# DeltaNet heads: the low weight part made from a negated high part and an accumulating transfer, in place of GpSimd's subtraction

## The reference

```
h = rmsnorm(x, norm_g)
proj = h @ w_in
(rq, rk, rv, rz, dq, dk, dv, dz, db, da, gr, gd) = split(proj)
o_r = retention(rope(rq), rope(rk), rv)      # normed, times silu(rz)
qkv = silu(causal_conv([dq, dk, dv], conv_w))
o_d = gated_deltanet(l2norm(q), l2norm(k), v, beta, g)   # normed, times silu(dz)
y = sigmoid(gr) * (o_r @ w_up_r) + sigmoid(gd) * (o_d @ w_up_d)
return x + y @ w_o
```

## Time and profile before

| | |
|---|---|
| median of 2 runs | 2645.55 us |
| span of the profiled execution, first to last instruction | 2644.2 us |
| TensorE busy | 2620.6 us (99%) |
| TensorE weight loads | 2238.1 us (85%) |
| VectorE busy | 1761.1 us (67%) |
| GpSimd busy | 798.6 us (30%) |
| ScalarE busy | 704.5 us (27%) |
| read from memory, written | 176.30 MB, 38.86 MB |

### The profile page before, as it was taken

How to read it: one execution, slowest core, us unless ns; L and a number is a source line. 1 busy time by engine, 2 the same in 40 slices (tenths; PEclk the granted TensorE clock), 3 DMA queues, 4 the chain that set the end, 5 groups by cost and what they waited for, 6 DMA issues and landing times.

```text
span 2644.2 us, 40210 instructions
## 1 busy us (share of the span) xinstructions
PE 2620.6 (99%) x14874; PEld 2238.1 (85%) x14874; DVE 1761.1 (67%) x3972; ACT 704.5 (27%) x1440; POOL 798.6 (30%) x451
## 2 busy tenths in 40 slices
PE   8999999999999999999999999999999999999998
PEld 6888888888888899888877888888888998898887
DVE  7878777877755555434577778777877555653333
ACT  5333333333311212200143333333332221231001
POOL 3123333333312212334512233332322122132453
PEclk9999999999999999999999999999999999999999
DMA  5321222122211112433533222222222111133344
GB/s 174 100 85 58 81 69 85 53 86 65 85 50 43 41 35 76 130 96 120 157 90 88 77 74 69 73 77 72 67 77 73 43 51 43 41 106 100 99 135 152
DMA packets 293416, 217.79 MB, mean 82 GB/s; under 512 B 31747, under 2 KB 246101, under 8 KB 292965
## 3 DMA queue, kind: packets, MB, share of 16 engines
q1 hardware_dynamic: 259620, 159.07, 20.9%
q10 hardware_dynamic: 33600, 56.15, 6.3%
HBM read 176.30 MB, written 38.86 MB: 81 GB/s over the span
## 4 chain that ended last, share of the span: by engine, by line
PE 92%; DVE 3%; DMA 2%; issue 1%; ACT 1%; SPq 0%; POOL 0%; ACTq 0%; DVEq 0%; POOLq 0%
PE dense_ps L866 23%; PE dense_ps L870 23%; PE dense_ps L868 23%; PE work L849 3%; PE dense_ps L890 2%; PE dense_ps L891 2%; PE dense_ps L892 2%; PE work L1145 1%; PE work L1182 1%; PE work L1202 1%; PE work L1121 1%; PE work L1104 1%; PE work L1171 1%; PE work L1195 1%; PE work L1156 1%
## 5 line engine op out<-in xcount | busy, mean ns | idle before, releaser
L866 PE MATMUL dense_ps<-act_hi,w_hi 128*128 128x512 f32 x2552 | 1048.3, 411 | 1.7 <-DVE w_lo L1797 0.8
L870 PE MATMUL dense_ps<-act_hi,w_lo 128*128 128x512 f32 x2552 | 998.4, 391 | 0.0
L868 PE MATMUL dense_ps<-act_lo,w_hi 128*128 128x512 f32 x2552 | 997.3, 391 | 0.0
L2579 POOL TENSOR_TENSOR w_lo<-w_raw,w_hi 128x1024 fp32r<-128x1024 f32 x162 | 400.1, 2470 | 1024.5 <-ACT w_hi L1429 582.7
L870 PEld LDWEIGHTS dense_ps<-act_hi,w_lo 128*128 128x128 f32 x2552 | 479.0, 188 | 105.8
L866 PEld LDWEIGHTS dense_ps<-act_hi,w_hi 128*128 128x128 f32 x2552 | 481.0, 188 | 86.9 <-POOL act_lo L2600 2.3
L868 PEld LDWEIGHTS dense_ps<-act_lo,w_hi 128*128 128x128 f32 x2552 | 481.5, 189 | 78.8 <-issue 0.5
L1973 DVE SCALAR_TENSOR_TENSOR arena<-arena,cols 128x512 f32<-128x512 f32 x288 | 244.3, 848 | 6.1
L1429 ACT ACTIVATE w_hi<-w_raw 128x1024 fp32r<-128x1024 f32 x94 | 99.1, 1054 | 330.5 <-PE dense_ps L870 310.5
L1419 ACT ACTIVATE arena<-dense_ps 128x512 f32<-128x512 f32 x96 | 57.2, 596 | 258.5 <-PE dense_ps L870 258.5
L849 PE MATMUL work<-mk,arena 128*128 128x128 f32 x768 | 112.1, 275 | 7.9 <-DMA arena<-in_x 7.9
(11 more groups left out here) (262 smaller groups left out, 4094.7 us busy)
## 6 DMA issues: line engine op xcount, KB each, us to landing
w_raw<-in_w_in SPq DMA_DIRECT2D x138, 512.0 KB, 3.8
arena<-l_scratch SPq DMA_DIRECT2D x64, 256.0 KB
arena<-gate_scratch ACTq DMA_DIRECT2D x64, 256.0 KB, 2.7
gate_scratch<-arena ACTq DMA_DIRECT2D x36, 256.0 KB, 2.0
w_raw<-in_w_out SPq DMA_DIRECT2D x18, 512.0 KB, 3.7
o_scratch<-arena ACTq DMA_DIRECT2D x32, 256.0 KB, 2.2
w_raw<-in_w_up_dn SPq DMA_DIRECT2D x16, 512.0 KB, 3.6
arena<-o_scratch ACTq DMA_DIRECT2D x32, 256.0 KB, 3.7
```

The lines of the kernel that those rows point to most:

```text
L866: eng.matmul(dense_ps[:, to, :], w_hi[:, slot, k, :], hi[:, k, seg], start=(k == 0), stop=False)
L868: eng.matmul(dense_ps[:, to, :], w_hi[:, slot, k, :], lo[:, k, seg], start=False, stop=False)
L870: mm = eng.matmul(dense_ps[:, to, :], w_lo[:, slot, k, :], hi[:, k, seg], start=False, stop=(k == KT - 1))
L2579: eng.tensor_tensor(w_lo[:, slot, :, :], w_from[second][:, :, :], w_hi[:, slot, :, :].bitcast(F32), ALU.subtract)\
```

## The change

In the units `even` and `odd` GpSimd's subtraction is replaced. ACT writes two things: `w_hi`, as before, and then, in a second instruction, `w_lo` from the same `w_raw` with scale -1. As `w_lo` has the short form too, that is the negated high part. GpSimd then issues a transfer that reads the raw block from memory again (`w_in`) and adds it to `w_lo` in place, which leaves raw - hi. It signals `w_lo_ok` as soon as the transfer is issued, which frees `w_raw` for the next load; the landing is told by two semaphores of their own (`w_added`, by the parity of the block), for which TensorE waits before the block's first matmul. `w_hi_ok` now counts two to a block, and all that waits for it is changed to match; the units `first`, `even_last` and `odd_last` and all other blocks keep the subtraction. Three signals of the gates are put on one semaphore (`Later`).

```diff
-        w_hi_ok, w_lo_ok = signal("w_hi_ready", 1), signal("w_lo_ready", 1)
+        w_hi_ok, w_lo_ok = signal("w_hi_ready", 2), signal("w_lo_ready", 1)
+        w_added = [plain("w_lo_added_even"), plain("w_lo_added_odd")]
...
-        b_tokps = signal("ba_tokens_psum", 1)
-        b_gcps, b_rowps, b_rows = signal("gc_psum", 1), signal("rows_psum", 1), signal("rows_ready", 2)
+        b_tokps, b_rows = signal("ba_tokens_psum_then_gc_then_rows", 3), signal("rows_ready", 2)
+        b_gcps, b_rowps = Later(b_tokps, 1), Later(b_tokps, 2)
...
                                 eng.wait_ge(w_lo_ok.sem, w_lo_ok.after(g, 1))
+                                if 1 <= g % NBLK - BLK_HEADS <= 6 * (DH - 1):
+                                    eng.wait_ge(*added(g))
...
+                def split_signed(g, slot):
+
+                    eng.wait_ge(w_in_ok.sem, w_in_ok.after(g, 16))
+                    eng.wait_ge(dense_ok[1].sem, dense_ok[1].after(g, -1))
+                    eng.wait_ge(w_hi_ok.sem, w_hi_ok.after(g, 0))
                     eng.activation(w_hi[:, slot, :, :], w_raw[:, :, :], ACT.Copy).then_inc(w_hi_ok.sem, 1)
+                    eng.activation(w_lo[:, slot, :, :], w_raw[:, :, :], ACT.Copy, scale=-1.0).then_inc(w_hi_ok.sem, 1)
...
+            def add_w(g, slot, col):
+
+                eng.wait_ge(w_hi_ok.sem, w_hi_ok.after(g, 2))
+                eng.dma_start(w_lo[:, slot, :, :], w_src(l, w_in, col), accum_op=ALU.add)\
+                   .then_inc(w_added[g % 2], 16)
+                eng.sem_inc(w_lo_ok.sem, 1)
...
                             if idx == BLK_RET + 2 and kind == "even_last":
                                 split_v(l, 0, 0)
+                            elif kind in ("even", "odd"):
+                                add_w(g + idx, idx % 2, head_column(h, idx - BLK_HEADS))
                             elif kind != "first" and not is_v(idx):
                                 split_w(g + idx, idx % 2)
```

More of the change, by code:

```diff
@@ L81, with __init__, Later @@
 class Signal:
-    def __init__(self, handle, per):
-        self.sem, self.per = handle, per
+    def __init__(self, handle, per, before=0):
+        self.sem, self.per, self.count = handle, per, before
     def after(self, t, k):
-        return t * self.per + (self.per + k)
+        return t * self.per + (self.per + self.count + k)
+def Later(first, before):
+    return Signal(first.sem, first.per, first.count + before)
 def constants():
@@ L621, in l_source, with head_column, added @@
                 .to_broadcast([NB, BASE, 2 * BASE * BASE])
+        def head_column(h, j):
+            if j == 6:
+                return DK0 + (h + 2) * P if h < DH - 2 else DZ0 + (h + 1) * P
+            return (None, DZ0 + h * P, DQ0 + (h + 1) * P, DV0 + (h + 1) * P, GD0 + (h + 1) * P, GR0 + (h + 1) * P)[j]
+        def added(g):
+            l, q = g // NBLK, g % NBLK - BLK_HEADS
+            assert 1 <= q <= 6 * (DH - 1)
+            return w_added[g % 2], 16 * len([1 for m in range(l + 1) for i in range(1, 6 * (DH - 1) + 1)
+                                             if m * NBLK + BLK_HEADS + i <= g and (m * NBLK + BLK_HEADS + i - g) % 2 == 0])
         def v_weights(h):
@@ L1428, in split_hi @@
                     eng.wait_ge(w_hi_ok.sem, w_hi_ok.after(g, 0))
+                    eng.activation(w_hi[:, slot, :, :], w_raw[:, :, :], ACT.Copy).then_inc(w_hi_ok.sem, 2)
+                def split_signed(g, slot):
+                    eng.wait_ge(w_in_ok.sem, w_in_ok.after(g, 16))
+                    eng.wait_ge(dense_ok[1].sem, dense_ok[1].after(g, -1))
+                    eng.wait_ge(w_hi_ok.sem, w_hi_ok.after(g, 0))
                     eng.activation(w_hi[:, slot, :, :], w_raw[:, :, :], ACT.Copy).then_inc(w_hi_ok.sem, 1)
+                    eng.activation(w_lo[:, slot, :, :], w_raw[:, :, :], ACT.Copy, scale=-1.0).then_inc(w_hi_ok.sem, 1)
                 def conv_tanh(t, i):
@@ L1554, in delta_unit @@
                             idx = g0 + step[1] + 1
-                            split_hi(g + idx, idx % 2)
+                            if kind == "first":
+                                split_hi(g + idx, idx % 2)
+                            else:
+                                split_signed(g + idx, idx % 2)
                         elif what == "tanh":
@@ L1790, in split_w @@
                     eng.wait_ge(dense_ok[1].sem, dense_ok[1].after(g, -1))
-                eng.tensor_copy(w_hi[:, slot, :, :], w_from[second is not None][:, :, :]).then_inc(w_hi_ok.sem, 1)
+                eng.tensor_copy(w_hi[:, slot, :, :], w_from[second is not None][:, :, :]).then_inc(w_hi_ok.sem, 2)
             def low_w(g, slot):
-                eng.wait_ge(w_hi_ok.sem, w_hi_ok.after(g, 1))
+                eng.wait_ge(w_hi_ok.sem, w_hi_ok.after(g, 2))
                 eng.wait_ge(w_lo_ok.sem, w_lo_ok.after(g, 0))
@@ L1811, in split_v @@
                 col = slice(j * P, (j + 1) * P)
-                eng.tensor_copy(hi[:, :, col], w_raw[:, :, :]).then_inc(w_hi_ok.sem, 1)
+                eng.tensor_copy(hi[:, :, col], w_raw[:, :, :]).then_inc(w_hi_ok.sem, 2)
                 if h == 0 and j == 1:
-                    eng.wait_ge(w_hi_ok.sem, w_hi_ok.after(g, 1))
+                    eng.wait_ge(w_hi_ok.sem, w_hi_ok.after(g, 2))
                     eng.wait_ge(w_lo_ok.sem, w_lo_ok.after(g, 0))
@@ L1823, in split_gates @@
                     eng.wait_ge(dense_ok[1].sem, dense_ok[1].after(g, -1))
-                eng.tensor_copy(w_hi[:, BLK_BA % 2, :, 0:16], w_raw[:, :, 0:16]).then_inc(w_hi_ok.sem, 2)
+                eng.tensor_copy(w_hi[:, BLK_BA % 2, :, 0:16], w_raw[:, :, 0:16]).then_inc(w_hi_ok.sem, 4)
             def norm_mean(t, b):
@@ L2585, in split_v @@
                 hi, lo = v_weights(h)
-                eng.wait_ge(w_hi_ok.sem, w_hi_ok.after(l * NBLK + BLK_RET + 6 * h + 2 + j, 1))
+                eng.wait_ge(w_hi_ok.sem, w_hi_ok.after(l * NBLK + BLK_RET + 6 * h + 2 + j, 2))
                 eng.tensor_tensor(lo[:, :, col], w_raw[:, :, :], hi[:, :, col].bitcast(F32), ALU.subtract)\
@@ L2590, in split_gates @@
             def split_gates(g):
-                eng.wait_ge(w_hi_ok.sem, w_hi_ok.after(g, 2))
+                eng.wait_ge(w_hi_ok.sem, w_hi_ok.after(g, 4))
                 eng.tensor_tensor(w_hi[:, BLK_BA % 2, :, 16:32], w_raw[:, :, 0:16],
```

## The result

| | before | after |
|---|---|---|
| median of the runs, us | 2645.55 | 2670.70 |
| lowest to highest, us | 2644.49 to 2646.61 | 2670.38 to 2671.02 |
| span of the profiled execution, us | 2644.2 | 2669.2 |

The ratio is 1.0093, with a 95% interval of 1.0064 to 1.0123: the change makes the kernel slower, by 25 us or 0.9%. That lies in the predicted range and in the forecast direction, but the loss is 25 us where 7 were forecast.

A forecast was written before the change was run, and what follows sets the result against it. The prediction took TensorE, 99% busy, to bound the kernel. Span 2644.2 + 7 (ACT's second copy) + 0 (transfer) = 2651, with 1.35 us from span to median 2652 us; range 2641 to 2760.

The forecast's parts named there:

- TensorE bounds the kernel: Whole kernel: TensorE is busy 99% of the span, so cuts elsewhere can give back no more than some 5 us.
- what is taken off GpSimd is worth nothing: GpSimd's 84 subtractions: 201 us of busy time go, off the path, worth 0 to TensorE.
- the transfer is in time: Accumulating transfer into `w_lo`: lands before its block's first matmul everywhere, costing 0; nothing lost up to 8.4 us.
- T: Time from the end of the second ACT copy to the transfer's landing: 7.0 us, bounds 4.4 to 15.7.
- the tightest space: Third block of each head: 8.4 us from the second copy's end to the block's start, 1.4 us in hand.
- Landing and accumulation: Parts of the transfer's time after the issue: 3.8 us for a plain landing plus 2.2 us for accumulating.
- "late transfer" rival: Third and sixth block of each head first: transfer lands late, 88 us at 12 us; over 53 us late, chance 0.29.
- the rival that GpSimd cannot issue while VectorE holds the port: Transfer issue: one hold costs 7 us (2659), more lead to late transfers; chance 0.17 together with slightly late, under 53 us.
- an estimate of 3.2 us for a plain transfer: Skill page's figure for 512 KB issued by GpSimd: about 2.0 us plus bytes over 436 GB/s; transfers then in time everywhere.
- the second copy holds `so`: ACT's copy to `vn` comes 1.05 us later, holding `so` some 0.55 us a head, 8 us; 7 taken, bounds 0 to 29.
- the hold on VectorE, put at 0: VectorE's tap L1970 no longer held by the subtraction: gives 0, at most 4.1 us; GpSimd's masks at most a little later.
- The likeliest case alone: No late transfer and a few us on ACT: 2641 to 2674 (0 and 29 us on ACT), chance 0.47.

The follow-up runs named there:

- Experiment 10: Changed kernel with GpSimd's masks ahead of the issue and each unit's first split as before, so 56 of 84 blocks use the transfer: 2645.61 us, ratio 1.0000.
- experiment 7: Changed kernel with a plain transfer from GpSimd instead of the accumulating one, so the subtraction is left out: 2661.04 us, ratio 1.0062.
- experiment 8: Changed kernel with each accumulating transfer split into two of 64 columns, twice the packets for the same bytes: 2689.22 us, ratio 1.0168.
- Experiment 4: Changed kernel with the negated copy of each unit's first split moved behind the first copy to `vn`: 2666.76 us, ratio 1.0082.
- experiment 5: Changed kernel with GpSimd's two masks put ahead of the issue of each unit's second transfer: 2654.68 us, ratio 1.0038.
- experiment 6: Changed kernel with GpSimd's masks ahead of each unit's second issue and the first split's negated copy behind the copy to `vn`: 2650.37 us, ratio 1.0023.
- experiment 1: Kernel before plus a negated ScalarE copy into `w_lo` ahead of the one to `w_hi`; GpSimd's subtraction stays, no transfer: 2673.43 us, ratio 1.0106.
- experiment 9: Kernel before plus the second ScalarE copy, with the two masks ahead of each unit's second subtraction, no transfer from GpSimd: 2671.07 us, ratio 1.0098.
- experiment 2: Changed kernel without the negated ScalarE copy, so the transfer adds onto what was in `w_lo`: 2653.34 us, ratio 1.0036.

## Why the prediction was right and wrong

*Right: TensorE bounds the kernel, and what is taken off GpSimd is worth nothing.* Experiment 10 frees GpSimd of 56 subtractions and is 0.5 us slower, which is inside its interval.

*Right, with luck: the transfer is in time.* The sum for T was 7.0; it measured 8.0, inside the bounds 4.4 to 15.7 and under the tightest space, 8.4. The issue was put at 1.0 and takes 1.57, and 0.3 us to its start were not in the sum. Landing and accumulation, 3.8 + 2.2 = 6.0 from the end of the issue, took 7.7 - 1.57 = 6.1, but by two errors that cancel: the plain transfer of experiment 7 takes 5.1 from there instead of 3.8, and accumulating adds 1.1 to it instead of 2.2. In the prediction's words 1.4 us in hand was thin; 0.4 were left in the median and 0.13 in the tightest block, where a start that waits comes 0.09 us after the landing (experiment 8). The "late transfer" rival did not come, nor did the rival that GpSimd cannot issue while VectorE holds the port: all 84 issues took between 1544 and 1728 ns. The Trainium skill, "DMA: Bandwidth & Descriptors", section "Anatomy of one DMA — SWDGE (gpsimd) path", stood for an estimate of 3.2 us for a plain transfer; experiment 7 has 6.0 for it.

*Right, with its size a little low: the second copy holds `so`.* 0.55 us a head and 8 us in all were worked out, 7 taken, and 9 measured. Experiment 4 shows the cause: with `vn` first the waits go. What this term is worth to someone who removes it is less, 2 to 6 us, since L1203, which waits for VectorE, is next.

*Wrong: the hold on VectorE, put at 0.* The step reads "It also stops holding VectorE", "But TensorE hardly waits for VectorE, so this gives 0", with GpSimd's masks "at most a little later". It is 14 of the 25 us. Half of it came true: of the three taps in a head that ran into a subtraction (1.62, 0.80 and 2.34 us), two are free in the kernel after, and TensorE gains nothing by it. But the third goes from 0.80 to 3.68 us, since the masks behind it now hold it. The position of the masks was not the error, as the first one begins 0.48 us behind the tap before and 0.23 after. What failed is that holds on VectorE were counted only as something that goes away; GpSimd's other work was not set against the same tap. Nor was the slack of its chain read, 1.26 us between L2263's end and L1145, which says that a hold of more than that costs TensorE time. The rows had the spread of this tap and the masks right behind the subtraction. That masks behind an issue hold it to the end of both they could not show, as no such issue stood in that trace. With the masks ahead of the issue (experiment 5) the term is gone.

*The range held for another reason than the one it was made for.* It reached to 2760 for a late transfer, which did not come. The likeliest case alone, 2641 to 2674, also holds the measured 2671, but by room given to the copy on ScalarE (0 to 29 us), of which 9 were used; 14 of the rest came from a term put at 0.

The sum as it should have read: ScalarE 9, VectorE held once a head, 14 in all, together 23, and a forecast of some 2669 us against 2671 measured. What this does not explain: in experiment 6, with both terms removed, 6.8 us remain. The profile shows 5.4 of them in the starts at L1203, behind VectorE. Experiment 10 lacks them, and it differs in the split of each unit's first block; which part of that split they hang on was not tried.

## What to carry to other kernels

Work on an engine that nobody waits for is not free of price: where two engines exclude each other and one of them feeds the bound, look at what stands beside the second one's steps before and after, also where nothing seems to move. A shift of a microsecond (experiment 1), or another kind of instruction in the same place (the change itself), is enough. A line whose longest run is several times its shortest marks such a place; find what it ran against, and ask what will stand there after the change. And removing the first of two waits in a chain gives back only the distance to the second, here about 4 us of 9.

## What the runs showed of the hardware

**GpSimd and VectorE exclude each other by instruction.** A `tensor_scalar` of VectorE from SBUF to SBUF in f32 waits for GpSimd's arithmetic: 465 ns free, up to 3703 ns with two masks; one with 4 columns 2.70 us instead of 0.17. A step with two inputs (`scalar_tensor_tensor`, 0.74 us free) is held too, by the subtraction (2.95 us, experiment 9) and by the masks (3.47 us, experiment 2). The Trainium skill, "SBUF — State Buffer", section "SBUF: two separate sides", calls the shared pair of ports an exclusive lock that whoever starts first keeps for its whole instruction, and the lengths agree with that. One thing does not fit: by the records the tap of the kernel after starts at 251.86, before the first mask at 252.09, and is still held to the end of the second. Starts on GpSimd are rough, so the order of 0.23 us proves little, and in one head of 14 the tap was free at the same distance. But where it was held behind an issue it was not let in between the two masks (here and in experiments 2 and 7), while in experiment 5 and in the kernel before it got in between two instructions of GpSimd. Why is open.

**An issue by GpSimd does not hold VectorE, and VectorE did not stretch it.** The tap took 0.47 us inside a pair of issues of 3.17 us (experiment 8), and 84 issues varied by 0.18 us. The same section says that such an issue gets no descriptors written while VectorE runs an instruction that takes both ports; no run here shows it.

**The price of an accumulating transfer of 512 KB in 1024 rows of 512 bytes.** Issue 1.57 us against 0.94 plain, landing 7.7 us against 6.0. As two transfers with half rows the pair of issues takes 3.17 us. The masks behind an accumulating issue are recorded at 1.93 and 1.89 us, overlapping with it and with each other, where behind a plain one they are 1.30 and 1.27: the issue's work seems to go on beside them, and it costs them time.
